# Emptying the projection banks ahead of a pair's last cast, and the recurrence's root one step later, in the two layers at the end of a 1-core kernel

## The reference

```python
for l in range(2):
    proj = rmsnorm(x, norm_g[l]) @ w_in[l]
    q, k, v, ga, iq, ik, iw, xr, gr, ma, mb = jnp.split(proj, offsets, axis=-1)
    attn = dsa_attention(rope(q), rope(k), v, rope(iq), rope(ik), iw)   # top 64 of the keys
    y_a = (attn * silu(ga)) @ w_out_attn[l]
    xr = causal_depthwise_conv_2(xr, conv_w[l], conv_b[l])
    hr = rg_lru(xr, w_rg[l], b_rg[l], w_ig[l], b_ig[l], lru_lambda[l])
    y_b = (hr * silu(gr)) @ w_out_rnn[l]
    x = x + (sigmoid(ma) * y_a + sigmoid(mb) * y_b) @ w_o[l]
```

## Time and profile before

| | us |
|---|---|
| median of three runs | 2176.56 |
| the profiled execution, its own time | 2177.72 |
| its span | 2175.9 |
| PE busy | 2124.5 (98%) |
| DVE busy | 1739.0 (80%) |
| ACT busy | 1488.5 (68%) |
| POOL busy | 394.1 (18%) |

### The profile page before, as it was taken

One profiled execution on the slowest core, in us unless ns is written; L12 is line 12 of the kernel. 1 busy time (PEld: TensorE's weight loads), 2 busy tenths in 40 slices (PEclk: granted clock), 3 DMA queues, 4 the chain that ended last, 5 costly groups with the idle time before them and its releaser, 6 DMA issues.

```text
span 2175.9 us, 35021 instructions
## 1 busy us (share of the span) xinstructions
PE 2124.5 (98%) x13875; PEld 1883.2 (87%) x13875; DVE 1739.0 (80%) x2158; ACT 1488.5 (68%) x1994; POOL 394.1 (18%) x354
## 2 busy tenths in 40 slices
PE   8999999989999999999999999999999999999998
PEld 8888999878888888888888888879898998899898
DVE  6756555878999999999999999975698665689676
ACT  5644444567887888888888888864687845477854
POOL 1511000001020000000000000000667500458710
PEclk9999999999999999999999999999999999999999
DMA  8325855429999999999999999965655465655553
GB/s 281 98 72 127 268 193 174 166 97 368 348 382 387 393 387 393 386 381 373 382 375 392 361 394 372 391 241 173 189 158 179 140 223 184 187 162 175 161 159 109
DMA packets 326676, 564.74 MB, mean 260 GB/s; under 512 B 19664, under 2 KB 160744, under 8 KB 326504
## 3 DMA queue, kind: packets, MB, share of 16 engines
q1 hardware_dynamic: 314576, 527.60, 68.9%
q0 software_dynamic: 11824, 34.77, 5.7%
q10 hardware_dynamic: 104, 0.04, 0.0%
HBM read 548.32 MB, written 14.02 MB: 258 GB/s over the span
## 4 chain that ended last, share of the span: by engine, by line
PE 80%; DVE 11%; ACT 5%; issue 2%; DMA 1%; SPq 1%; DVEq 0%; ACTq 0%; POOLq 0%
PE bank L945 24%; PE bank L947 24%; PE bank L946 24%; DVE parts L2769 4%; PE bank L951 2%; PE bank L1111 1%; ACT parts L2047 1%; DVE work L3587 1%; ACT work L2655 1%; PE bank L1944 1%; PE bank L1904 1%; DVE work L3590 0%; DMA work<-scr_hr 0%; ACT bank L2646 0%; DVE work L3588 0%
## 5 line engine op out<-in xcount | busy, mean ns | idle before, releaser
L2769 DVE TENSOR_TENSOR parts<-raw,parts 128x1024 fp32r<-128x1024 f32 (+2 forms) x709 | 856.5, 1225 | 309.0 <-ACT parts L2047 283.7
L2047 ACT CAST parts<-raw 128x1024 fp32r<-128x1024 f32 (+2 forms) x709 | 729.4, 1037 | 398.0 <-PE bank L947 377.0
L945 PE MATMUL bank<-cols,parts 128*128 128x256 f32 (+1 forms) x1632 | 473.2, 290 | 4.8 <-DVE work L3700 4.8
L946 PE MATMUL bank<-cols,parts 128*128 128x256 f32 (+1 forms) x1632 | 462.3, 283 | 0.0
L947 PE MATMUL bank<-cols,parts 128*128 128x256 f32 (+1 forms) x1632 | 462.3, 283 | 0.0
L2769 DVE TENSOR_TENSOR fast<-raw,fast 128x1024 fp32r<-128x1024 f32 x302 | 361.8, 1219 | 24.2 <-ACT fast L2047 7.0
L2047 ACT CAST fast<-raw 128x1024 fp32r<-128x1024 f32 x302 | 316.4, 1052 | 84.3 <-PE bank L947 78.2
L945 PEld LDWEIGHTS bank<-cols,parts 128*128 128x128 f32 (+1 forms) x1632 | 312.6, 192 | 11.5 <-DVE parts L2769 5.8
L946 PEld LDWEIGHTS bank<-cols,parts 128*128 128x128 f32 (+1 forms) x1632 | 312.6, 192 | 2.8 <-issue 1.9
L947 PEld LDWEIGHTS bank<-cols,parts 128*128 128x128 f32 (+1 forms) x1632 | 312.5, 191 | 0.0
L945 PE MATMUL bank<-parts,cols 128*128 128x512 f32 x740 | 292.3, 395 | 3.2 <-DVE cols L2816 1.9
(11 more groups left out here) (458 smaller groups left out, 3437.7 us busy)
## 6 DMA issues: line engine op xcount, KB each, us to landing
raw<-in_moe_w_gate_dram SPq DMA_DIRECT2D x112, 1024.0 KB, 8.8
raw<-in_moe_w_up_dram SPq DMA_DIRECT2D x112, 1024.0 KB, 8.6
raw<-in_moe_w_down_dram SPq DMA_DIRECT2D x112, 1024.0 KB, 9.1
raw<-in_w_in_dram SPq DMA_DIRECT2D x76, 1024.0 KB, 5.3
raw<-in_a_w_in_dram SPq DMA_DIRECT2D x11, 1024.0 KB, 11.7
raw<-in_ffn_w_gate_dram SPq DMA_DIRECT2D x11, 1024.0 KB, 5.3
raw<-in_ffn_w_up_dram SPq DMA_DIRECT2D x11, 1024.0 KB, 5.3
raw<-in_ffn_w_down_dram SPq DMA_DIRECT2D x11, 1024.0 KB, 5.0
```

What stands on the lines that cost most here:

```text
L945: pe.matmul(o, l[0], r[0], start=start, stop=False)
L946: pe.matmul(o, l[0], r[1], start=False, stop=False)
L2047: a.copy(dst[0], src).then_inc(*up(o + "hi", x))
L2769: v.tensor_tensor(dst[1], src, dst[0].bitcast(F32), ALU.subtract).then_inc(*up(o + "lo", x))
```

## The change

Three edits, each in ACT's or DVE's written order. First, `fm` gets `bank_first`: the cast (or subtraction) that the pair's last tile frees is issued behind the emptying of the bank and not ahead of it. Second, this is switched on for gr and ma on ACT, and for gr on DVE (for ma DVE has no emptying). Third, in ACT's recurrence one of the two yields moves ahead of the root, so that a block's gates and decays lie in one step and its root in the next.

```diff
-        def fm(tiles, evac, ticks=0, pace=None, also=None, pairs=iter(())):
+        def fm(tiles, evac, ticks=0, pace=None, also=None, pairs=iter(()), bank_first=False):
             n = len(tiles)
             for nb, i in enumerate(range(0, n, 2)):
                 m = min(2, n - i)
-                for j in range(m):
+                for j in range(m - 1 if bank_first else m):
                     after(tiles[i + j])
                     if j + 1 < m:
                         tick(ticks // 2)
                 evac(i, m, nb, tiles[i + m - 1])
+                if bank_first:
+                    after(tiles[i + m - 1])
                 next(pairs, None)
...
                             k.then_inc(*up(name, l, n))
+                        yield
                         a.wait_ge(*at("rnn_tanh", l, n))
                         a.activation(TH[:, h:h + 2, :], TH[:, h:h + 2, :], ACT.Sqrt).then_inc(*up("rnn_root", l, n))
-                        yield
                         yield
...
-                fm(t_["gr"], tanh_to(L2.GR, "gr_th", 2, [(f"xr_out{i}", l) for i in range(3)]), ticks=2, also=rn)
-                fm(t_["ma"], tanh_to(L2.MA, "ma", 2), ticks=2, pairs=rn)
+                fm(t_["gr"], tanh_to(L2.GR, "gr_th", 2, [(f"xr_out{i}", l) for i in range(3)]), ticks=2, also=rn, bank_first=True)
+                fm(t_["ma"], tanh_to(L2.MA, "ma", 2), ticks=2, pairs=rn, bank_first=True)
...
-                fm(t_["gr"], silu(L2.GR, "gr", 2), ticks=2, also=rn)
+                fm(t_["gr"], silu(L2.GR, "gr", 2), ticks=2, also=rn, bank_first=True)
```

More of the change, by code:

```diff
@@ L2774, in after, with fm @@
                     lo(W_, o, y)
-        def fm(tiles, evac, ticks=0, pace=None, also=None, pairs=iter(()), behind=0):
+        def fm(tiles, evac, ticks=0, pace=None, also=None, pairs=iter(()), behind=0, bank_first=False):
             n = len(tiles)
```

## The result

The changed kernel takes 2163.17 us (median of six runs, 2162.54 to 2165.71), and the kernel before, run beside it, 2177.53 (2175.59 to 2179.5). The ratio is 0.9932, with a 95% interval of 0.9922 to 0.9941: 14.4 us less, where 9.6 were forecast. (The forecast starts from the 2176.56 of the first three runs of before; from there it is 13.4.) The profiled execution took 2162.74 us, and its span is 2160.9, 15.0 less than before.

A forecast was written before the change was run, and what follows sets the result against it. PE, busy 98% of the span, was taken as the bound. Gains of 5.4 or 5.3 and 5.1 us in the two layers, less 0.4 each for POOL, made 9.6: 2176.56 to 2167.0 us, range 2164.6 to 2172.

The forecast's parts named there:

- the prize: PE's idle columns from v's second half to the output, over both layers: 11.3 us, all that the change could win.
- Part 1, the head start: End of v: the later root takes 1.83 us off ACT's path, DVE starts 1.83 earlier, and PE's 0.4 goes.
- the head start is lost: Rival: DVE starts no earlier at the end of v; 6.9 us gained in all, 2169.7 us; chance 0.22.
- Part 1, behind gr: Attention's transposes: later roots shorten ACT's path to probabilities and copies; PE's waits of 1.03, 1.19 and 0.64 us go.
- The close meetings at line 3683: DVE's use of the root, blocks 3 to 6: for block 3 the root ends at 1649.3, DVE comes at 1649.8.
- Part 2: gr on DVE: one subtraction goes behind the first silu, which comes 1.7 us earlier; with DVE's earlier start, PE's 2.35 goes.
- POOL's meetings: DVE's moved stretch in gr may be blocked by POOL at the shared port: 0.4 us charged a layer, range 0 to 1.1.
- hr's path: From ma's last tile to block 7: +0.5 at block 6, +1.28 at mb, -1.3 at block 7; +0.5 in sum.
- The limit by POOL's convolution of block 7: POOL's convolution ends 0.75 us ahead of PE's gates and comes some 4.6 earlier, so PE may gain about 5.3.
- Given back at yb: Rival: hr comes no earlier, or ACT's unchanged number of table loads only moves PE's wait; 2176.2 us; chance 0.14.
- Slower: Rival: DVE waits for the roots of blocks 0 to 3, losing 5.5 us up to gr; 2181.8 us; chance 0.06.
- The signs: Wrong if DVE idles for the root in ga or gr, yb's wait grows, or gr's third pair still waits for DVE.

The follow-up runs named there:

- the early roots: The whole change, but with the yield moved only for the roots of blocks 0 to 2: 2170.89 us, ratio 0.9967 to the kernel before.
- the late roots: The whole change, but with the yield moved only for the roots of blocks 3 to 7: 2165.67 us, ratio 0.994 to the kernel before.
- banks alone: The kernel before with only the first two edits (bank ahead of cast in gr and ma), without the moved yield: 2174.59 us, ratio 0.9985.
- block 7's old root: The whole change, except that the root of block 7 stays in its old place: 2168.05 us, ratio 0.995 to the kernel before.
- roots only: The kernel before with only every block's root moved a step later, banks emptied in the old order: 2165.64 us, ratio 0.9946.

## Why the prediction was wrong

The direction was right and so was the mechanism in the main; the size was not: 2163.17 lies below the low end, 2164.6.

- **The step that failed** is the prize, "everything gained is 11.3". I took PE's idle column for what a wait costs. The same waits cost 14.3 us: 0.13 to 0.23 more than their column at each of 11 waits, 2.2 in all, and 0.3 a layer behind the fifth transposes, where the list of waits names nothing, as at block 2's gates, worth 0.2 a layer more. The low end was built on this number, so it could not hold a change that worked in full. The rows that show it were in the trace of before.
- **Part 1, the head start.** DVE starts 3.22 us earlier, of which 1.31 is PE's own lead at that point in this execution; the rest, 1.9, answers to the 1.83. POOL's wait went, and only where the early roots moved. That the transposes needed the head start was wrong: with the edits in gr, the late roots do without. Hence the gain under "the head start is lost" was put too low: 6.9 us, where the kernel with the late roots won 12.4 in the layers.
- **Part 1, behind gr.** 1.03, 1.19 and 0.64 went with blocks 3 to 7, worth 3.73 a layer. The close meetings at line 3683 came out as forecast, with 0.4 us of DVE's time at blocks 4 and 7 and no wait of PE for it in the list.
- **Part 2.** The silu gained 2.2 us, not 1.7: the subtraction that left was the one that POOL held. I had halved the pair's 3.43, though the two are not alike. ACT's part in gr and ma is worth nothing, as charged.
- **POOL's meetings**, charged with 0.4 a layer, went the other way, from 17 to 9. Their end at nothing was in the range.
- **hr's path.** From the matmul behind PE's fifth transposes to the end of block 7's scan it takes 37.74 and 37.69 us before, and 37.82 and 38.49 after: +0.1 in the first layer, where +0.5 was forecast, and +0.8 in the second. Block 7's own gain, forecast at 1.3, is 1.6 in the first layer of its experiment. The limit by POOL's convolution of block 7 was forecast at a gain of 5.3 for PE. In the first layer it did not bind, at a gain of 7.2: the convolution ends at 1709.58 and PE's gates start at 1710.88, 1.30 us of slack for 0.75 before. In the second it did bind, at 7.0: the gates start 0.05 us behind the convolution's end, and PE lost 0.21 us there against before, too little for the list of waits (the same befell the first layer of the kernel without DVE's edit in gr):

```profile
2058.27 1.08 POOL L908 TENSOR_TENSOR work<-work 88x506 f32<-88x506 f32 x1
```

```profile
2059.40 0.88 PE L1944 MATMUL bank<-work 88*88 88x256 f32 x3
```

At yb PE gave back 0.05 us in the first layer; in the second it won 0.33 there, 0.13 less than three other kernels. That it gave back so little was in part luck: hr's way out and back was a microsecond shorter in the second layer (14.0 for 15.0), which no edit explains. In the two kernels without ACT's part in gr or in ma, which differ from the whole change at yb alone, the layers hold 13.9 and 14.4.

- **The sum again**: 9.6, and 1.7 for the returns that hardly came, make 11.3; with 2.8 that the columns left out, 14.1; 0.2 more is rounding (the columns sum to 11.5), which gives the 14.3. With 0.4 at block 2's gates, less 0.2 at block 7's and the little at yb, that is the 14.5 of the layers.
- **The rivals.** "Given back at yb" is what banks alone do in the first layer, and what block 7's old root starts. With all roots moved it does not happen. The rule by the number of table loads has no support: all three traces (before, after, roots only) have 58, and the place alone was worth 10.7 us. "Slower" had it right that DVE comes to wait for the root, but not in the full stretch (blocks 0 to 3 show no such wait), and its size did not come.
- **The signs.** All that would have shown it wrong stayed away: DVE's 0.4 us at block 4 lie behind gr. Of those for it, DVE's idle time at the end of v is 3.21 and not about 4.0, and the wait for hr's last split, which was to stand in both layers, stands in no list.

What stays open: when a subtraction beside POOL's scaling (line 904) is held. Most are not, and some are, ending 0.61 to 0.63 us behind it. In part the scaling was the one that was late: in before, ten subtractions ran at their own 1.21 to 1.23 us wholly inside a scaling, and those scalings took 1.96 to 2.83 us, where the shortest took 0.92. Open is also why POOL's convolution of block 7 came some 1.4 us later against PE in after's second layer than in its first, and what makes hr's way out and back vary from 13.7 to 15.3 us over the 20 layers profiled here. At yb that decides over the better part of a microsecond a layer.

## What to carry to other kernels

Price a wait of a pipelined engine from start to start, less the steady distance between two instructions; the idle column leaves out the overlap, and 11 short waits made that 2.2 us here. Before halving a pair of instructions, look at each of the two and at what stood beside the longer one: moving a single subtraction out of the shadow of another engine's instruction won nearly twice its own length. Before saying whether two edits add, compare them place by place. In the layers roots alone won 10.7 us, banks alone 1.7, both 14.5. Up to the last transposes that is 11.2, 3.7 and 14.4: the two nearly add, since at gr's third pair both shorten the same wait (1.0 and 2.2 of 2.6), and at the transposes banks alone give back 0.4 a layer. The other 2.5 us lie at yb, where an earlier PE meets hr, and hr's way out and back alone differs by up to 1.6 us.

## What the hardware showed beyond that

A subtraction on DVE (two operands in SBUF) that began inside POOL's two-operand addition ended 1.08 or 1.09 us after it in all 17 cases of the first trace, so it waited for the addition's end (in the second in 9 of 13, and the other four began in the addition's last 0.08 us); DVE's silu, with one operand in a PSUM bank, took 0.67 us inside the same addition. A table load took 1.28 us, and in these kernels it cost PE only where the next result that PE wanted stood behind it on ACT.
